# Two transformer blocks in one kernel: a table of convolution taps per portion, and new orders of portions around the attentions

## What is computed

```python
q, k, v, up, ca, cb = project_inputs(h, w_in[l], q_norm_g[l], k_norm_g[l])
attn = diff_attn_post(diff_attention(q, k_all, v_all, lam), subln_g[l], lambda_init)
pool_o = pool_mixer(up, pool_w[l], pool_scale[l])
conv_o = conformer_conv(ca, cb, conv_dw_w[l], conv_dw_b[l], conv_ln_g[l], conv_ln_b[l])
mix = jnp.concatenate([attn, pool_o, conv_o], axis=-1)
x = x + g1 * jnp.einsum('blm,md->bld', mix, w_out[l])
x = x + g2 * swiglu(modulate(rms_norm(x, norm2_g[l]), sh2, sc2), w_ffn_in[l], w_ffn_out[l])
```

## Time and profile before

| what | value |
|---|---|
| median of 3 runs | 1629.23 us (1628.46 to 1630.73) |
| profiled execution, its own time | 1626.78 us |
| its span | 1625.0 us |
| TensorE matmuls busy | 1573.7 us, 97% |
| TensorE weight loads busy | 1456.5 us, 90% |
| VectorE busy | 1137.7 us, 70% |
| ScalarE busy | 921.4 us, 57% |
| GpSimd busy | 126.5 us, 8% |
| mean granted TensorE clock | 0.999 |

### The profile page before, as it was taken

The page is one execution under the profiler, slowest core; times in us unless marked ns, Lnnn a source line. Parts: engine busy times, 40 slices in busy tenths (PEclk is TensorE's granted clock), DMA queues, the critical chain, the costliest instruction groups (busy, mean ns, idle before and its releaser), DMA issues. The chain is left out here.

```text
span 1625.0 us, 31033 instructions
## 1 busy us (share of the span) xinstructions
PE 1573.7 (97%) x12856; PEld 1456.5 (90%) x12856; DVE 1137.7 (70%) x1782; ACT 921.4 (57%) x1462; POOL 126.5 (8%) x104
## 2 busy tenths in 40 slices
PE   6999999999999999998999999999999999999999
PEld 4887479999999999965899999878999998789999
DVE  5798677645566555897765556787887568788873
ACT  4444756635464444647554446776666467766662
POOL 0410000211001100300011100000101000001110
PEclk9999999999999999999999999999999999999999
DMA  9442765665546555435577654233555543235553
GB/s 395 166 182 104 284 261 205 240 239 219 196 166 227 188 192 196 157 130 188 212 228 237 208 202 162 94 110 106 209 191 198 209 149 102 102 131 187 205 204 110
DMA packets 46204, 304.38 MB, mean 187 GB/s; under 512 B 5072, under 2 KB 7408, under 8 KB 12784
## 3 DMA queue, kind: packets, MB, share of 16 engines
q1 hardware_dynamic: 45488, 301.21, 51.5%
q0 software_dynamic: 288, 0.92, 0.1%
q10 hardware_dynamic: 288, 0.27, 0.0%
HBM read 299.23 MB, written 3.15 MB: 186 GB/s over the span
## 5 line engine op out<-in xcount | busy, mean ns | idle before, releaser
L2062 DVE TENSOR_TENSOR wl<-raw,wh 128x1040 fp32r<-128x1040 f32 (+1 forms) x472 | 578.4, 1264 | 299.2 <-ACT wh L1820 236.0
L1820 ACT ACTIVATE wh<-raw 128x1040 fp32r<-128x1040 f32 (+1 forms) x472 | 468.8, 1035 | 188.8 <-PE bank L1610 112.8
L1605 PE MATMUL bank<-hx_hi,wh 128*128 128x256 f32 x1856 | 518.5, 279 | 5.4 <-ACT hx_hi L1820 3.2
L1610 PE MATMUL bank<-hx_lo,wh 128*128 128x256 f32 x1856 | 515.1, 278 | 0.0
L1608 PE MATMUL bank<-hx_hi,wl 128*128 128x256 f32 x1856 | 514.0, 277 | 0.3 <-DVE wl L2062 0.2
L1605 PEld LDWEIGHTS bank<-hx_hi,wh 128*128 128x128 f32 x1856 | 348.7, 188 | 11.1 <-issue 10.8
L1608 PEld LDWEIGHTS bank<-hx_hi,wl 128*128 128x128 f32 x1856 | 348.7, 188 | 2.7 <-issue 1.9
L1610 PEld LDWEIGHTS bank<-hx_lo,wh 128*128 128x128 f32 x1856 | 348.6, 188 | 0.7 <-DVE hx_lo L2055 0.4
L1608 PE MATMUL bank<-hid_hi,wl 128*128 128x256 f32 x912 | 252.2, 276 | 1.4 <-DVE wl L2062 1.4
L1605 PE MATMUL bank<-hid_hi,wh 128*128 128x256 f32 x912 | 252.5, 277 | 0.4 <-ACT wh L1820 0.3
L1610 PE MATMUL bank<-hid_lo,wh 128*128 128x256 f32 x912 | 251.9, 276 | 0.0
(11 more groups left out here) (219 smaller groups left out, 1880.6 us busy)
## 6 DMA issues: line engine op xcount, KB each, us to landing
raw<-in_wts SPq DMA_DIRECT2D x208, 1032.0 KB, 4.8
raw<-in_wts SPq DMA_DIRECT2D x50, 1024.0 KB, 6.5
raw<-in_wts SPq DMA_DIRECT2D x26, 776.0 KB, 4.3
tscr<-tmp SPq DMA_DIRECT2D x4, 512.0 KB, 7.3
bias<-tscr SPq DMA_DIRECT2D x4, 512.0 KB, 5.9
xTc<-in_ctxT SPq DMA_DIRECT2D x1, 1024.0 KB, 5.0
xTx<-in_xT SPq DMA_DIRECT2D x1, 1024.0 KB, 8.1
out_x<-xTx POOLq DMA_DIRECT2D x3, 256.0 KB, 2.6
```

Source lines behind the costliest of these rows:

```text
L1605: pe.matmul(out, block(f, M.wh, w0 + k, ncols, c, m), x_hi, start=first and k == 0 and o == 0, stop=False, skip_group_check=True)
L1610: ins = pe.matmul(out, block(f, M.wh, w0 + k, ncols, c, m), x_lo, start=False, stop=last and k == nk - 1, skip_group_check=True)
L1820: return act.activation(out, in_, func, bias=bias, scale=scale)
L2062: tt(M.wl[k][:, cols], M.raw[r][:, cols], M.wh[k][:, cols].bitcast(F32), ALU.subtract).then_inc(*on.inc(lo))
```

## The change

The pump of each portion takes its second number from a table TAPS, by layer, stream and position in the list of parts, in place of the rule 2 or 8. All three order strings are new. They hold the same portions the same number of times, but for `h`, `s` and `t`: in IN_FIRST 9 `h` and 2 `s` become 24 `h`, 3 `t` become 10; in IN_SECOND 11 `h` become 23, 1 `t` becomes 11; in BETWEEN 28 `h` become 39. Three asserts are added; they run while the program is written and issue nothing.

```diff
-IN_FIRST = ("G", "G m m", "", "G m", "h G G", "m", "m m", "t h", "x c m", "S N m", "m m s h m A", "", "m m",
-            "t T h m s h Y", "m Z h O O m", "O h h h m m", "O m", "", "t m", "m")
-IN_SECOND = ("h P K K h h", "m h h", "h P", "m S x h m h h", "", "m N A", "m Z m", "P t O h", "m", "", "h m O", "")
-BETWEEN = ("r D0 L2 L0 N r h D2 r h D4 r D3", "", "D1 r r", "Q0 K0", "", "r h r Q1 K1", "h V", "D5", "h h h h",
-           "h h r r Q2 h h Q3 h", "", "K2 r h r h r K3", "h h h h", "h r O0 h O1 O2", "", "", "", "O3 h", "h",
-           "h h h T0 h T1 T2 T3 h")
+IN_FIRST = ("G", "G h h", "t m G", "t", "m", "m t t G", "m G h", "m", "m h h t x h h c", "m", "m N t m h m h A m h",
+            "", "t h m h m", "T m h Y h", "t m t O O h S h m", "h h O h Z m h t m h h", "O m", "", "m", "h h m")
+IN_SECOND = ("K h t P", "h t m h h K", "h t h P x m", "t h h N S A Z h m h m", "", "m", "t t m", "P h t t t h t h h",
+             "m m", "h h", "h O h h h h h", "O t h")
+TAPS = {(0, "c"): (8, 10, 4, 12, 14, 12, 8, 0, 4), (0, "x"): (10, 8, 10, 6, 8, 8, 10, 10, 6),
+        (1, "c"): (12, 10, 10, 2), (1, "x"): (2, 8, 14, 14, 2, 0, 6, 6, 10)}
+BETWEEN = ("r D0 h L0 L2 N h r h r D2 D4 h r D3", "", "r D1 h r", "Q0", "K0", "r h h h V", "h h r Q1", "h K1 D5", "h",
+           "Q2 h h r r h Q3 h", "h h", "h r K2 r r h K3", "h h h", "h h h h h h h h r h O0 O1 O2", "", "", "", "h O3",
+           "h", "h h T0 h h T1 T2 T3 h")
...
     def inproj1(l, streams, toks, parts):
-        for part in parts:
+        for n, part in enumerate(parts):
...
-                pooling = part == "p" or part == "q0" and s == streams[0]
                 pump(2)
                 run_pending()
-                pump(2 if pooling else 8)
+                pump(TAPS[(l, s)][n])
                 project1(l, s, part, bank, tk)
```

More of the change, by code:

```diff
@@ L1375, in mla_values @@
         def mla_values(f):
+            assert len(ck_toks) == 2
             for j in range(2):
@@ L1451, in values @@
                 mla, v = u > 3, u % 4
+                assert not mla or len(v_toks) == 2
                 step("val2", mla=mla, u=v, pT=pT2, ready=[st_[2 * u], st_[2 * u + 1], v_toks if mla else dil[4 + v // 2]],
```

## The result

The change makes the kernel slower. The changed kernel takes 1640.74 us (median of 6 runs, 1638.71 to 1642.57) beside 1629.98 us for the kernel before on the same chip (6 runs, 1628.44 to 1632.29): +10.8 us, ratio 1.0067, 95% interval 1.0054 to 1.0079. The forecast was 1622.5 us, so the sign was wrong, and 1640.74 lies outside the range, which ended at 1637. Of the rivals, (a), with 1636.2 us, comes nearest.

The account below looks back on a forecast made before the run. TensorE, busy 97% of 1625.0 us, was taken as the bound, with 29.3 us of idle time as ceiling. Terms +1.5 - 1.5 - 1.5 - 1.7 - 2.5 - 1.0 = -6.7 us took the median 1629.23 to 1622.5 us; range 1610 to 1637.

Parts of the forecast that it names:

- (a): Rival: taps beside GpSimd's pooling delay the weights; layer 0 +6, layer 1 +2.5, 1636.2 us; chance 0.25.
- k0's halves: Layer 0, weight halves: 18 taps beside the pooling make k0's first half 2.5 us late for TensorE.
- the same account: Late halves add nothing to the first unit's wait, as a TensorE held up earlier waits less there.
- VectorE loses nothing net: Layer 0: moving taps beside the pooling costs VectorE nothing net, since before it was loaded beside POOL too.
- The first unit: Layer 0, first attention unit's weights: TensorE waits 3.4 us in place of 1.9, +1.5 us, bounds -1.9 and +12.
- The rest of layer 0: Layer 0's other 5.0 us idle: split portions and `h` ahead of output pieces gain -1.5 us, bounds -3 and +1.
- Layer 1: Layer 1 taps: the first unit's wait falls from 2.31 to 0.8 us, -1.5 us, bounds -2.3 and +1.5.
- The half of v0: Layer 1: 12 more taps make v0's first half 2.5 us late, inside the first unit's wait.
- The transfer: A piece's transfer moves with its splits on SP; priced at nothing, but without that cover ScalarE's halves wait.
- The units after: Layer 1, units after the first: half of the 2.12 + 2.88 us waits goes, -2.5 us, bounds -5 and +2.
- The clock: Between 722 and 728 us: the 1.2 GHz stretch goes with the wait, -1.7 us, bounds -1.7 and +1.7.
- Second block: Second block: portions spread and `h` moved gain -0.5 us per layer, -1.0 in the sum, bounds -1.5 and +1.5.

Follow-up runs that it names:

- e6: Kernel after, layer 0's 18 extra taps moved from before v0's half to the next four portions, still 124 before the first unit's weights: +8.9 us shift from 118 to 255.
- e14: Kernel before with 12 layer 0 taps moved from after the pooling to beside it, still 102 ahead of the first unit's weights: ratio 1.0004.
- e13: Kernel before with 22 more layer 0 taps ahead of the first unit's weights, all after the pooling's end: 9.6 us of waits in place of 1.9.
- e7: Kernel before with one IN_FIRST edit, the projection of k1 of x with its ten taps one unit earlier: shift 4.4 us.
- e1: Kernel before with the new TAPS table alone, order strings as before: 12.1 us slower by the medians, ratio 1.0071.
- e9: Kernel after with 30 layer 0 taps moved behind the first maximum, still 124 ahead of the first unit's weights: 1642.4 us.
- e4: Kernel before with the new BETWEEN and nothing else: 12 runs between 1626.67 and 1634.56 us.
- e8: Kernel before with 8 fewer taps in layer 0's k1 of c and 6 fewer in layer 1's v1 of c, issued later: ratio 1.0004.
- e10: Kernel before with layer 0's k1 of x one unit up, eight of its taps and modulation pieces behind it; layer 1 taps thinned, one modulation piece later: 1647.18 us.
- e12: Kernel before with layer 0's k1 of x one unit up, eight of its taps and modulation pieces behind it; in layer 1 only Z one entry later: ratio 0.9993.
- e15: Kernel before with 24 layer 1 taps of x moved forward to beside the pooling, number ahead of the first unit unchanged: 1628.06 us.

## Why the prediction was wrong, point by point

**k0's halves, right.** 2.5 us late was forecast, 2.91 us waited. That such lateness comes out of the same account as the first unit's wait held with 124 taps ahead (e6), not with 102 (e14: 0.64 us late, and the 1.88 us wait stays). That VectorE loses nothing net beside the pooling was nearly right: some 1.5 us in e14, 1.2 in the kernel after.

**The first unit, the step that failed.** The term was +1.5 us, and three things in it were wrong. First, the idle time. The prediction put the weights' end at 143.8 us, since VectorE's idle 2.8 us would take part of the 8.9, TensorE at 140.4, and so 3.4 us in place of 1.9: +1.5. In the kernel after they end at 145.8, 8.1 us later than in before, and in e13 the same 22 taps move them by 8.8. So the idle time took 0.8 us in place of 2.8, for two reasons. 1.78 us of it was a wait for ScalarE's half of k0. Ten of the new taps stand ahead of that half and do fill it in the kernel after, but the taps beside the pooling give some 1.2 us of it back (an estimate: 8.14 later, 1.78 filled and 0.13 from an earlier start, less 22 x 0.404 = 8.89). In e13 the taps stand behind it, and it stays idle. The other 1.0 us is not free either: 0.60 us is one more wait for ScalarE, at 130.8 us in before and at 142.2 in the kernel after.

Second, TensorE did not get to the cover. It stopped in the kernel after at the scores of the third unit, 140.45 us, which need a bank that the first exponential frees, which needs the first maximum: 138.71 us in place of 127.31. The prediction counted taps up to the weights and none up to that maximum. Third, the cover was taken from the next unit (e7).

In waits, 2.91 + 2.44 us stand where 1.88 stood, +3.5 for the +1.5. With two stretches at 1.2 GHz and shorter waits the term comes to some 8 us: the shift goes from -0.2 us at 79 us to 8.0 at 181, where both kernels have again issued the same matmuls. e13 shows that the number of taps is enough for such a loss (11.4 us of shift from these 22 taps alone, e1 10.8), and e6, e9 and e14 that their place is not what costs.

**The rest of layer 0, right in sign only.** -1.5 was forecast, "roughly the 1.06 us wait". That wait is still there (1.07 us at 211.15 us); another became shorter (1.35 us at 184.3 us in before, 0.72 at 191.7), and the shift falls from 8.0 at 181 us to 7.4 at 255: -0.6.

**Layer 1.** The 2.31 us wait at the first unit is gone, with one of 0.49 ahead of it, as forecast. The half of v0 was not late as forecast: its 14 taps ran at 0.40 us, since GpSimd's first sum was held in their place, and the lateness came one half later. But "paid out of the same account" failed here: 1.64 and 3.05 us came before the first unit. The transfer that the prediction priced at nothing, with the words that ScalarE's halves wait if its cover is gone, is on that chain. The units after, forecast at -2.5 us, have 1.88 + 1.91 + 1.16 + 2.10 = 7.1 us of waits where 2.12 + 2.88 = 5.0 stood: +2.1. TensorE's idle time from 695 to 805 us, which was to be near 8 us, is 14.1 (704.30 to 817.00 in the kernel after) in place of 13.4.

**The clock.** -1.7 us was forecast, bounds of 1.7 either way, for a single stretch. There are four, each after a wait of 2.1 to 3.05 us, and over all runs the clock costs some 2.6 us more than before. Whoever forecasts waits of over 2 us has to add the clock to each.

**Second block.** -1.0 was forecast, +1.7 came; alone the new BETWEEN has it too (e4, 1.6).

Rival (a) had the ratio of the layers about right (+6 and +2.5 against +7.6 and +4.6) for another reason than it gave: in layer 0 its taps beside the pooling cost little, and its condition that VectorE is full already was nearly the whole of it. Its 0.25 should have been the largest chance, as 0.404 us x 22 was the one large number in the sum and only 1.5 of it was charged.

## What to carry to other kernels

Where an engine is full up to the moment that another needs its result, count what is put ahead of that moment: each instruction delays it in full, wherever it stands, and the engine's idle moments don't take it up unless they lie behind it and are free. Test first whether taking work away helps (e8): if not, the wait is a chain and the queue is merely full to the brim. And find the first result that frees a buffer, not the one that the consumer reads: the cover planned for the second is never reached if the first is late. Here, though, putting the first in time moved the wait and did not shorten it (e9), since the work ahead of the second was the same.

## What the runs showed of the hardware

The granted clock follows the length of TensorE's waits loosely. Over the 18 traces (from 30 us on, the last few us left out) a stretch at 1.2 GHz began between 1 us before the wait and 4 us after it in this many cases:

```
wait of TensorE     waits   with a stretch at 1.2 GHz
1.2 to 1.5 us        17      0
1.5 to 2.0 us        61     15
2.0 to 2.4 us        44     22
over 2.4 us          25     24 (one in a stretch that had begun before)
```

The one exception is the 2.88 us wait of the kernel before at 751.8 us. The same wait (1.9 us at 138 us) kept 2.4 GHz in one execution and lost it in another (before, e4), and three stretches (two near 204 us in e10 and e12, one at 760 us in e12) followed no single wait over 1.1 us.

Beside the same VectorE work a GpSimd instruction can be held or not: the first sum of layer 1's pooling took 8.27 us in the kernel after, while 14 taps ran in their 0.40 us each, and 1.23 us in e15, where the 14 taps took 0.92 each. In both it started 0.60 us after the first of these taps (676.81 after 676.21, 669.51 after 668.91). With the 16 taps behind them both come to the same total (5.64 + 13.61 and 12.82 + 6.41 us, 19.2 each).
